# Down matrices loaded from Pool's queue, gate-and-up from SP's, in an MoE encoder layer on one Trainium2 core

## The reference

```python
mod = (cond @ ada_w[i] + ada_b[i])[:, None, :]
sh1, sc1, g1, sh2, sc2, g2 = jnp.split(mod, 6, axis=-1)
hm = rms_norm(x, norm1_g[i]) * (1.0 + sc1) + sh1
y = diff_attention(hm, da_w_in[j], da_w_out[j], ...)
x = x + g1 * y
hf = rms_norm(x, norm2_g[i]) * (1.0 + sc2) + sh2
x = x + g2 * hierarchical_moe(hf, ...)
...
def block(args):            # one expert e on its tokens
    xb, e = args
    g, u = jnp.split(xb @ w_gu[e], 2, axis=-1)
    return (jax.nn.silu(g) * u) @ w_d[e]
```

## Time and profile before

| | us |
|---|---|
| Time, median of 3 runs (lowest to highest) | 1600.62 (1599.5 to 1601.64) |
| Span of the profiled execution | 1598.7 |
| PE busy | 1164.8 (73% of the span) |
| DVE, ACT, POOL busy | 626.6, 149.6, 111.3 |
| Mean granted TensorE clock | 0.88 of full |
| DMA | 577.75 MB, mean 361 GB/s |
| of it SP's queue (hardware_dynamic) | 474.37 MB |
| of it Pool's queue (software_dynamic) | 102.77 MB |

### The profile page before, as it was taken

The page is one execution under the profiler, slowest core; times in us unless marked ns, Lnnn a source line. Parts: engine busy times, 40 slices in busy tenths (PEclk is TensorE's granted clock), DMA queues, the critical chain, the costliest instruction groups (busy, mean ns, idle before and its releaser), DMA issues.

```text
span 1598.7 us, 20914 instructions
## 1 busy us (share of the span) xinstructions
PE 1164.8 (73%) x8438; PEld 757.4 (47%) x8438; DVE 626.6 (39%) x1109; ACT 149.6 (9%) x354; POOL 111.3 (7%) x143
## 2 busy tenths in 40 slices
PE   2298899999998998867657558657557557657655
PEld 1286788888886887424224224224113223223211
DVE  6476766666874012454214114214213213213213
ACT  3000411212222011100000000000000000000001
POOL 4232111111111000100000000000000000000000
PEclk9598999999997998988879888779878888788877
DMA  9997999999994644899999999999999999999995
GB/s 315 348 349 258 348 371 365 368 313 304 375 375 159 229 158 158 342 414 407 412 414 413 413 414 414 413 414 415 413 413 416 412 413 415 413 413 415 414 412 227
DMA packets 183544, 577.75 MB, mean 361 GB/s; under 512 B 10278, under 2 KB 75980, under 8 KB 166604
## 3 DMA queue, kind: packets, MB, share of 16 engines
q1 hardware_dynamic: 156604, 474.37, 76.5%
q0 software_dynamic: 26896, 102.77, 17.9%
HBM read 575.02 MB, written 2.10 MB: 361 GB/s over the span
## 4 chain that ended last, share of the span: by engine, by line
PE 47%; DMA 36%; SPq 7%; DVE 6%; another core or an unknown queue 1%; issue 1%; ACT 1%; DVEq 0%; POOL 0%; ACTq 0%; POOLq 0%
DMA ring<-in_moe_w_gu_dram 25%; PE psum L492 10%; PE psum L607 7%; PE psum L673 7%; SPq L318 6%; DMA ring<-in_moe_w_d_dram 6%; PE psum L502 5%; PE psum L649 4%; DMA ring<-in_da_w_in_dram 4%; PE psum L722 4%; PE psum L702 3%; DVE arena L938 2%; PE psum L533 2%; SPq L321 1%
## 5 line engine op out<-in xcount | busy, mean ns | idle before, releaser
L673 PE MATMUL psum<-ring,ada_ring 128*32 128x256 f32 x4000 | 305.2, 460 | 197.0 <-DMA ring<-in_moe_w_gu_dram 196.8
L673 PEld LDWEIGHTS psum<-ring,ada_ring 128*32 128x32 f32 x4000 | 139.2, 128 | 360.0 <-DMA ring<-in_moe_w_gu_dram 254.8
L938 DVE SCALAR_TENSOR_TENSOR arena<-ada_ring,silu_c,arena 128x512 f32<-128x512 f32 x360 | 270.6, 752 | 28.2 <-DMA ada_ring<-in_ada_w_dram 16.6
L702 PE MATMUL psum<-ring,arena 128*32 128x512 f32 x1024 | 161.0, 770 | 34.3 <-DMA ring<-in_moe_w_d_dram 22.3
L492 PE MATMUL psum<-region_b,ring 128*128 128x256 f32 x768 | 167.8, 379 | 0.0
L1234 DVE TENSOR_SCALAR arena<-arena 128x128 f32<-128x128 f32 x32 | 7.2, 227 | 389.0 <-ACT arena L862 389.0
L492 PEld LDWEIGHTS psum<-region_b,ring 128*128 128x128 f32 x768 | 145.0, 190 | 19.2
L1245 DVE TENSOR_TENSOR arena<-psum,arena 32x512 f32<-32x512 f32 x112 | 76.9, 687 | 186.1 <-PE psum L702 183.4
L375 POOL DMA_DIRECT2D ada_ring<-in_ada_w_dram x128 | 98.0, 768 | 368.3 <-DVE arena L938 361.0
L607 PE MATMUL psum<-ring,region_a 128*128 128x256 f32 x512 | 115.3, 387 | 0.9 <-ACT region_a L790 0.9
L607 PEld LDWEIGHTS psum<-ring,region_a 128*128 128x128 f32 x512 | 98.9, 194 | 15.5 <-ACT region_a L790 1.3
(11 more groups left out here) (197 smaller groups left out, 713.2 us busy)
## 6 DMA issues: line engine op xcount, KB each, us to landing
ring<-in_moe_w_gu_dram SPq DMA_DIRECT2D x125, 2048.0 KB, 25.1
ring<-in_moe_w_d_dram SPq DMA_DIRECT2D x64, 2048.0 KB, 23.4
ada_ring<-in_ada_w_dram POOLq DMA_DIRECT2D x64, 1024.0 KB, 9.8
ring<-in_da_w_in_dram SPq DMA_DIRECT2D x24, 2048.0 KB, 27.8
ada_ring<-in_ada_w_dram POOLq DMA_DIRECT2D x64, 512.0 KB, 9.7
ring<-in_da_w_out_dram SPq DMA_DIRECT2D x8, 2048.0 KB, 24.9
region_a<-in_x_dram SPq DMA_DIRECT2D x1, 2048.0 KB, 12.1
region_b<-in_x_dram POOLq DMA_DIRECT2D x1, 2048.0 KB, 7.8
```

What stands on the lines that cost most here:

```text
L673: last = mm(psum[32 * n:32 * n + 32, B_GU, 0:256].rearrange("p (a b) -> p a b", a=2), x_items[:, k, SLOTS * i:SLOTS * (i + 1)], w[:, kk, : ...
L702: last = mm(psum[32 * n:32 * n + 32, B_D + i % 2, :], hid_t[:, k, :], w[:, kk, n, :], start=k == 0, stop=k == FT - 1)
L938: ins = v.scalar_tensor_tensor(out=acc[:, par, :], in0=w, scalar=silu_c[:, k:k + 1], in1=acc[:, par, :], op0=ALU.mult, op1=ALU.add)
```

## The change

SP's `load_item` becomes `load_gu` and issues only j = 0 to 3. Pool gets `load_d`, which issues j = 4 and 5 into the same slots, under the same `slot_free` counts, ahead of which it waits in its own program: items 0 and 1 after the second load of x and ahead of the waits for the two diagonal matrices, item 2 after these, items 3 to 31 in a loop, and a copy of the loop for extra items. Down has landing semaphores of its own, one for each j, for item 0 (`first_d_loaded`) and for the others (`next_d_loaded`); PE waits for them at L698. The counts for gate-and-up (`moe_loads`) are adapted: a slot whose content alternates between gate-and-up and down in the beginning counts one load less. Ring, slots, order of use on PE, bytes and arithmetic stay.

```diff
         def moe_loads(m, j):
-            return m + (moe_at(m, j) // RING + 1)
+            behind_first_d = not (isinstance(m, int) and m == 0) and j < 2
+            return m + (moe_at(m, j) // RING + (0 if behind_first_d else 1))
+        def d_loaded(m, j):
+            return (first_d_loaded if is_first(m) else next_d_loaded)[j - 4]
+        def d_loads(m):
+            return 16 if is_first(m) else m * 16
...
-            def load_item(m, e):
-                gu, dn = w_gu(e), w_d(e)
-                for j in range(RING):
+            def load_gu(m, e):
+                gu = w_gu(e)
+                for j in range(4):
                     if isinstance(m, int) and (m, j) in SPARE:
                         continue
                     sp.wait_ge(w_used, slot_free(m, j))
                     s = moe_slot(m, j)
...
-            load_item(0, 0)
+            load_gu(0, 0)
             sp.wait_ge(w_used, MOE_CH0)
             load_spare(sp, 2)
-            load_item(1, 1)
-            load_item(2, 2)
+            load_gu(1, 1)
+            load_gu(2, 2)
             with sp.Fori(3, EXPERTS) as m:
-                load_item(m, m)
+                load_gu(m, m)
...
             gp.dma_start(x_res, x[0].rearrange("(a p) d -> p a d", p=P)).then_inc(x_again, 16)
+            def load_d(m, e):
+                dn = w_d(e)
+                for j in (4, 5):
+                    gp.wait_ge(w_used, slot_free(m, j))
+                    s = moe_slot(m, j)
+                    gp.dma_start(ring[:, s, :].rearrange("p (k n) -> p k n", k=2),
+                                 dn[:, 2 * (j - 4):2 * (j - 4) + 2, :]).then_inc(d_loaded(m, j), 16)
+            load_d(0, 0)
+            load_d(1, 1)
             gp.wait_ge(w_used, MOE_CH0 + RING + 1)
             gp.wait_ge(mod_ready, 24)
...
                 .then_inc(diag_ready, 1)
+            load_d(2, 2)
+            with gp.Fori(3, EXPERTS) as m:
+                load_d(m, m)
...
-                        pe.wait_ge(w_loaded[s], moe_loads(m, j) * 16)
+                        pe.wait_ge(d_loaded(m, j), d_loads(m))
```

More of the change, by code:

```diff
@@ L182, in encoder_layer @@
         spare_loaded = [sem(f"spare_loaded{i}") for i in range(len(SPARE))]
+        first_d_loaded = [sem(f"first_d_loaded{i}") for i in range(2)]
+        next_d_loaded = [sem(f"next_d_loaded{i}") for i in range(2)]
         w_used = sem("w_used")
@@ L241, in moe_loads, with is_first @@
         def moe_loads(m, j):
-            return m + (moe_at(m, j) // RING + 1)
+            behind_first_d = not (isinstance(m, int) and m == 0) and j < 2
+            return m + (moe_at(m, j) // RING + (0 if behind_first_d else 1))
+        def is_first(m):
+            return isinstance(m, int) and m == 0
+        def d_loaded(m, j):
+            return (first_d_loaded if is_first(m) else next_d_loaded)[j - 4]
+        def d_loads(m):
+            return 16 if is_first(m) else m * 16
         def slot_free(m, j):
@@ L316, in load_item @@
                     s = moe_slot(m, j)
[L317 to L322, removed]
-            load_item(0, 0)
+                    sp.dma_start(ring[:, s, :].rearrange("p (k n) -> p k n", k=4),
+                                 gu[:, 4 * j:4 * j + 4, :]).then_inc(w_loaded[s], 16)
+            load_gu(0, 0)
             sp.wait_ge(w_used, MOE_CH0)
             load_spare(sp, 2)
-            load_item(1, 1)
-            load_item(2, 2)
+            load_gu(1, 1)
+            load_gu(2, 2)
             with sp.Fori(3, EXPERTS) as m:
-                load_item(m, m)
+                load_gu(m, m)
             sp.wait_ge(tables_ready, 1)
@@ L339, in _ @@
                             e = sp.value_load(extra_i[0:1, bass.ds(g * QUAD + j, 1)], min_val=0, max_val=EXPERTS - 1)
-                            load_item(g * QUAD + (EXPERTS + j), e)
+                            load_gu(g * QUAD + (EXPERTS + j), e)
                     sp.end_ifs()
@@ L400, in _ @@
                 .then_inc(diag_ready, 1)
+            load_d(2, 2)
+            with gp.Fori(3, EXPERTS) as m:
+                load_d(m, m)
+            gp.wait_ge(tables_ready, 1)
+            extra_groups = gp.value_load(extra_i[0:1, EXTRA:EXTRA + 1], min_val=0, max_val=EXTRA // QUAD)
+            with gp.If(extra_groups > 0):
+                with gp.Fori(0, EXTRA // QUAD) as g:
+                    with gp.If(g < extra_groups):
+                        for j in range(QUAD):
+                            e = gp.value_load(extra_i[0:1, bass.ds(g * QUAD + j, 1)], min_val=0, max_val=EXPERTS - 1)
+                            load_d(g * QUAD + (EXPERTS + j), e)
+                    gp.end_ifs()
+            gp.end_ifs()
         @block.tensor
```

## The result

| | before | after |
|---|---|---|
| Time, median (lowest to highest) | 1600.06 (1598.47 to 1601.64), 4 runs | 1628.38 (1624.32 to 1629.48), 4 runs |
| Ratio to before, 95% interval | 1 | 1.0167 (1.0149 to 1.0186) |
| Span of the profiled execution | 1598.7 | 1622.7 |
| Bytes on SP's queue, on Pool's | 474.37, 102.77 MB | 340.15, 236.99 MB |

A forecast was written before the change was run, and what follows sets the result against it. Transfers at 414 GB/s bound the kernel, 30.4 us per expert. Tail 9.9, six group ends 16.2, first group end 10.0 and item 2 1.0 sum to +37.1 us: 1637.7 us on the median, range 1609 to 1650.

The forecast's parts named there:

- Rate unchanged: DMA transfers in the expert stage: two full queues move data at the same 414 GB/s as one.
- Shares of two to one: While both queues have work, down's 8 KB packets against gate-and-up's 4 KB give down two thirds of the rate.
- Nothing left of the down waits but item 2's: TensorE's 22.3 us of waits for down go, except about 10 us in item 2, with no gain in time.
- Tail: Kernel end: gate-and-up's fourth chunk lands last, leaving 11.86 us of work after it instead of 1.97, +9.9 us.
- three signs of being wrong: Steady rate between group ends not 414 GB/s, no dips there, or down landing after the fourth gate-and-up chunk.
- Six group ends: The six later group ends: DMA engines run dry 2.7 us at each, +16.2 us in all.
- The reserve: Six outstanding chunks keep transfers going after TensorE stops using chunks, for 28.0 us after the last landing.
- First group end: After the first four experts: DMA engines dry 10.5 us where 0.5 was, +10.0 us.
- The late item 2: Item 2's down, loaded late by Pool, makes TensorE wait some 10 us, at no cost as five chunks are outstanding.
- Item 2: Between item 2's gate-and-up and SP's next issue nothing is queued: 0.8 us dry, taken as +1.
- Only the tail: Rival, chance 0.12: the group ends stay bridged and only the kernel's end costs, at the least 1610.5 us.
- Slower or faster mixing: Rivals for every expert: two queues slow transfers (1647 us, chance 0.08) or speed them past 431.5 GB/s (1595.5, chance 0.08).

The follow-up runs named there:

- one-queue kernel: The kernel before, all loads on SP's queue, with each item's two down chunks issued ahead of its fourth gate-and-up chunk: 1641.8 us, ratio 1.0261.
- the second: A second profile of the unaltered changed kernel, run again as reference for other kernels: median 1626.9 us, ratio 1.0158 to the kernel before.
- the order repaired: The changed kernel with the down chunks of each group's last item (3, 7, ... 31) back on SP's queue behind gate-and-up: 1609.5 us, ratio 1.0061.
- the last repair: The changed kernel with down of each group's last item and of item 2 back on SP's queue: 1603.0 us, ratio 1.0012.

## Why the prediction was right, and where its terms were off

The forecast was 1637.7 us, +37.1, range 1609 to 1650; measured 1628.4, +28.3. Sign, range and mechanism held; the size was nearly a third too large (37.1 for 28.3).

- *Rate unchanged.* Right: 413 to 414 GB/s with both queues in use. The rule of the Trainium skill that I had set beside it ("DMA: Bandwidth & Descriptors", Latency and other measured facts: engines 7 and 15 slower, tied, as a best guess, to rings of Pool's queue) did not show in the rate; single engines were not looked at.
- *Shares of two to one.* Right, 0.85 to 0.40 MB.
- *Nothing left of the down waits but item 2's.* Right, and no gain came of it.
- *Tail, forecast 9.9, measured 5.9 (4.6 became 10.5 us).* The step that failed is that gate-and-up's last chunk lands with the last byte. Pool issued the last item's down late, and down's bytes ended last (1591 to 1594 us: Pool's packets only). "Down lands after the fourth gate-and-up chunk" was one of the three signs of being wrong: in the last item it is so, without a wait of TensorE for it. Before, down's second landing was seen 2.7 us after the mean end of the bytes; now gate-and-up's fourth was seen 2.8 us ahead of it, 5.5 us less. Against that, TensorE needed 13.3 us behind that landing, at a mean clock of 0.53, where I had 11.86, at 0.74: 9.9 - 5.5 + 1.4 = 5.8. Where gate-and-up's fourth chunk did land last, in the one-queue kernel, the tail is 14.2, 9.6 more than before, so the price was right. The last item's down removed from Pool gave 6.8 back.
- *Six group ends, forecast 16.2.* Measured 11.7. Their time from the landing to the next used chunk was well forecast: 28.9, and 28.5 to 30.1, mean 29.3, in the profile. The reserve was mis-sized: 29.3 + 1.8 us to the bytes, less 11.7 / 6 = 1.95 lost, is 29.2, where I had 28.0 from one dip and a landing inferred behind it. That is 1.2 us too little, six times, 7 us; the longer time from landing to use gave some 2.5 of them back.
- *First group end, forecast +10.0.* Measured +8.7 and +12.5. That the size was near is in part luck. From the fourth landing to the next used chunk I had 36.7 us, and it was 34.1 in the first profile and 37.5 in the second; the reserve, which I had at 28.0, was only 34.1 + 1.8 - 9.3 = 26.6 and 37.5 + 1.8 - 13.1 = 26.2 there, and no run shows why it is shorter than the 29.2 at the six others. In the first profile the two errors cancel.
- *The late item 2.* "That costs nothing, as five chunks are outstanding" held in the changed kernel, where DVE waited 5.35 us for item 3's SwiGLU after its table. But I had followed the late down to PE and to the DMA engines, not to DVE, where 19.5 us of copying and planning start with item 2's output. With the order repaired, this lateness alone still left 9.4 us dry, and the order alone made a dip of 11.2 us with one queue: two causes, each enough for the whole dip, of which the second is hidden as long as the first is there. No run has the changed order with item 2 in time, as the order itself makes item 2 late.
- *Item 2, forecast +1.0.* As a dip of its own it is 0.2 us (the slice of 394 GB/s at 680 us).
- *The rivals.* "Only the tail" is out, by the dips; its price of 1610.5 us also left out the first group end, whose 7.6 us at the least it could not avoid. Slower or faster mixing is out, by the rate of 413 to 414 GB/s and by the last repair, with 23 of 32 items' down still on Pool's queue.

What stays open: why TensorE had the lower clock at the first group end in one execution and not in the other, why the reserve is shorter there, and why Pool issues the last item's down late.

## What to carry to other kernels

In a kernel bound by transfers, ask what work stands behind the landing that comes last, not how long any load waits. A load that arrives earlier than it is needed gave nothing here, and if it overtakes what is needed first, the engine's whole remaining item comes behind the last landing and is taken from the ring's reserve: look for the places where the engine stops using chunks (group ends, the end of the kernel) and compare that time, from the last landing to the next issue, with what the ring holds. When a step becomes late, follow it to every engine that starts something long behind it, not just to the one that waits.

## What the runs showed of the hardware that was not expected

When both queues are full the engines take packet for packet (108 of Pool's and 97 of SP's in 3 us), so that the queue with the larger packets has the larger share (0.85 to 0.40 MB). An early load of 4 MiB on Pool's queue put off the landing that mattered by some 11 us: 696.18 for 684.06, in an item that began 0.9 us later than before.

With one queue TensorE began on the last chunk 2.7 us (before) and 1.4 us (one queue, new order) after the mean end of the bytes, and the reserve of the same ring came out at 26.2 to 29.2 us by place. So it is better taken from a dip of the rate at the place in question than from landings alone.
